# Attention of the second block's layers: heads in pairs, weights on the probabilities, outputs already turned

## The reference

```python
for l in range(2):
    h = rms_norm(x, norm_mix[l]) * (1 + sc_m) + sh_m
    (q_a, kc_a, vc_a, ks_a, vs_a, kw_a, vw_a, g_a, q_b, k_b, v_b, g_br) = split(h @ w_in[l])
    y_a = nsa_mixer(...)    # 8 query heads, 2 key/value groups, three branches:
    #   compressed: softmax(q @ k_c.T * 64**-0.5) @ v_c, 15 compressed keys (blocks of 32 tokens, stride 16)
    #   selected:   here all blocks are picked, so causal softmax(q @ k_slc.T * 64**-0.5) @ v_slc
    #   window:     window 512 > 256, so causal softmax(q @ k_win.T * 64**-0.5) @ v_win
    #   out = g[0] * o_c + g[1] * o_s + g[2] * o_w     (a sigmoid gate per token and head)
    y_b = moba_mixer(...)   # 8 heads with keys of their own, causal softmax over the 256 tokens
    merged = gate_a * (y_a @ w_up_nsa[l]) + gate_b * (y_b @ w_up_moba[l])
    x = x + g_m * (merged @ w_out[l])
    x = x + g_f * ffn(...)
```

## Time and profile before

| | us |
|---|---|
| median of 3 runs | 2434.91 (2433.66 to 2440.22) |
| the profiled execution | 2438.09 |
| its span | 2436.2 |
| TensorE busy | 2034.8 (84%) |
| VectorE busy | 411.6 (17%) |
| ScalarE busy | 325.4 (13%) |

### The profile page before, as it was taken

How to read it: one execution, slowest core, us unless ns; L and a number is a source line. 1 busy time by engine, 2 the same in 40 slices (tenths; PEclk the granted TensorE clock), 3 DMA queues, 4 the chain that set the end, 5 groups by cost and what they waited for, 6 DMA issues and landing times.

```text
span 2436.2 us, 28154 instructions
## 1 busy us (share of the span) xinstructions
PE 2034.8 (84%) x12190; PEld 1308.8 (54%) x12190; DVE 411.6 (17%) x1137; ACT 325.4 (13%) x737; POOL 0.2 (0%) x4
## 2 busy tenths in 40 slices
PE   6999997766656666666666699989999999899999
PEld 4468786421111111221111347878888658788887
DVE  4213343200000000000000114431000114411000
ACT  2232020200000000000000112431000122501000
POOL 0000000000000000000000000000000000000000
PEclk9999998888787788888788899899999999999999
DMA  9247577599999999999999954216334545045341
GB/s 327 77 165 271 197 267 285 210 422 427 430 428 429 428 428 429 428 429 427 430 428 429 411 195 157 86 70 242 138 127 168 192 138 208 1 173 207 136 175 35
DMA packets 147872, 648.48 MB, mean 266 GB/s; under 512 B 10645, under 2 KB 17410, under 8 KB 123016
## 3 DMA queue, kind: packets, MB, share of 16 engines
q1 hardware_dynamic: 140754, 643.00, 66.6%
q10 hardware_dynamic: 7030, 4.18, 0.7%
HBM read 646.10 MB, written 1.05 MB: 266 GB/s over the span
## 4 chain that ended last, share of the span: by engine, by line
PE 62%; DMA 31%; DVE 3%; ACT 2%; issue 1%; ACTq 1%; SPq 0%; DVEq 0%
DMA ring<-in_w_exp 31%; PE bank L806 27%; PE bank L820 6%; PE bank L2268 6%; PE bank L1601 4%; PE bank L1365 4%; PE bank L1616 2%; PE bank L577 1%; PE bank L839 1%; PE bank L684 1%; DMA ring<-in_w_branch_ml 1%; ACTq L346 1%; PE bank L1289 1%; PE bank L2074 1%; PE bank L2067 1%
## 5 line engine op out<-in xcount | busy, mean ns | idle before, releaser
L806 PE MATMUL bank<-hx,ring 128*128 128x256 f32 (+1 forms) x2944 | 655.1, 385 | 0.7 <-ACT hx L702 0.7
L806 PEld LDWEIGHTS bank<-hx,ring 128*128 128x128 f32 x2944 | 559.4, 190 | 93.3 <-issue 19.0
L1601 PE MATMUL bank<-ring,arena 128*32 128x512 f32 x1968 | 307.3, 759 | 201.8 <-DMA ring<-in_w_exp 191.4
L1601 PEld LDWEIGHTS bank<-ring,arena 128*32 128x32 f32 x1968 | 60.8, 124 | 430.9 <-DMA ring<-in_w_exp 310.0
L1616 PE MATMUL bank<-ring,arena 128*32 128x512 f32 x1008 | 159.9, 774 | 83.5 <-DMA ring<-in_w_exp 72.7
L820 PE MATMUL bank<-ring,hx 128*128 128x512 f32 (+1 forms) x384 | 152.9, 560 | 1.1 <-ACT hx L762 0.7
L2268 PE MATMUL bank<-arena,ring 128*128 128x256 f32 x704 | 152.4, 379 | 1.5 <-DVE arena L2301 1.5
L2268 PEld LDWEIGHTS bank<-arena,ring 128*128 128x128 f32 x704 | 133.6, 190 | 20.0 <-issue 1.9
L1616 PEld LDWEIGHTS bank<-ring,arena 128*32 128x32 f32 x1008 | 32.3, 130 | 193.6 <-DMA ring<-in_w_exp 114.5
L820 PEld LDWEIGHTS bank<-ring,hx 128*128 128x128 f32 x384 | 72.8, 190 | 80.1 <-issue 76.4
L1659 DVE COPY arena<-bank 128x256 f32<-128x256 f32 x16 | 6.8, 424 | 523.1 <-PE bank L1606 523.1
(11 more groups left out here) (370 smaller groups left out, 1542.3 us busy)
## 6 DMA issues: line engine op xcount, KB each, us to landing
ring<-in_w_exp SPq DMA_DIRECT2D x186, 2048.0 KB, 16.2
ring<-in_w_ada SPq DMA_DIRECT2D x36, 2048.0 KB, 12.4
ring<-in_w_in SPq DMA_DIRECT2D x29, 2048.0 KB, 9.1
ring<-in_w_ffn_in SPq DMA_DIRECT2D x20, 2048.0 KB, 7.9
ring<-in_w_ffn_out SPq DMA_DIRECT2D x10, 2048.0 KB, 7.8
ring<-in_w_out SPq DMA_DIRECT2D x6, 2048.0 KB, 12.0
arena<-in_w_exp SPq DMA_DIRECT2D x4, 2048.0 KB, 16.1
ring<-in_w_up_nsa SPq DMA_DIRECT2D x2, 2048.0 KB, 9.4
```

The source lines that it names most:

```text
L806: ins = pe.matmul(b[:, o:o + n], w[:, k, j * P:(j + 1) * P], h[:, k, :], start=k == 0, stop=k == KD - 1)
L1601: ins = pe.matmul(banks[s][32 * j:32 * j + 32, :], e_xe[:, 2 * t + kk, :], w[:, kk, 512 * j:512 * j + 512], start=t + kk == 0, stop=t + kk ...
```

## The change

- The unit is a pair of heads (`par` = 0, 1) of one branch: 12 units, the four pairs of the third branch first, then the other two branches of each pair.
- Keys are kept as pairs like the queries (`kT`). A head's scores are a matmul over its own 64 partitions; the two heads of a pair write to two banks.
- The scale 64**-0.5 is put into the query gains, so that `softmax_in` gives the exponential's bias directly (minimum of the negated scores); L2190 goes.
- New `normed(m)` on VectorE between `probs` and `turned`: reciprocal of the sums, times the gate, and four multiplies of the probabilities in place.
- `values` has the value columns as weights (64 columns) and the turned probabilities moving, so that the output is already turned. The two heads write the two halves of the partitions of one bank, and the three branches of a pair add up in that bank. `outputs` is a plain copy to `yT2`.
- One copy in six of the turned probabilities goes to VectorE (`on_dve`).
- The compressed scores are made turned (32 rows of keys a head, four pairs side by side), copied, turned back, softmaxed and weighted, turned again as one bank, and their values are added behind the window branch of each pair. The compressed values are made in four 32-partition copies.
- The opening's order is, on TensorE: scores(0), compressed scores, scores(1), their turn, turned(0), scores(2), turned(1), values(0), scores(3), turn of the compressed probabilities; on VectorE: softmax_in(0), softmax_in(1), compressed softmax, normed(0), softmax_in(2), compressed sums and weights, normed(1).
- `y2`, its turn and its copies go.

```diff
@@ heads
-                for par in range(2):
-                    lo, hi = 64 * par, 64 * par + 64
-                    s0 = par if q == 2 else 8 + par
-                    v.tensor_copy(kp[lo:hi, s0:s0 + 7:2, c * P:(c + 1) * P], bb[lo:hi]).then_inc(*DV.step("free " + key, f"kp{l}"))
+                s0 = 4 if q == 2 else 0
+                v.tensor_copy(kT[:, s0:s0 + 4, c * P:(c + 1) * P], b[:, :].rearrange("p (i t) -> p i t", i=4)).then_inc(
+                    *DV.step("free " + key, f"kT{l}"))
@@ TensorE
+    UNITS = [(2, p) for p in range(4, 8)] + [(b, p) for p in range(4) for b in range(2)]
+        def scores(m):
+            b = [bank(pe, f"s{l}_{m}{par}") for par in range(2)]
+            for c in range(NC):
+                for par in range(2):
+                    r = slice(64 * par, 64 * par + 64)
+                    o = slice(0, P) if c == 0 else slice(P, 3 * P)
+                    ins = pe.matmul(b[par][:, o], qT[r, pair, c * P:(c + 1) * P], kT[r, slot_, 0:(c + 1) * P],
+                                    start=True, stop=True)
+                    if c:
+                        ins.then_inc(*PE.step(f"full s{l}_{m}{par}"))
+        def turned(m):
+            for par in range(2):
+                b = bank(pe, f"pt{l}_{m}{par}")
+                pe.wait_ge(*at(f"N{l}_{m}{par}"))
+                for i in range(3):
+                    ins = pe.transpose(b[:, i * P:(i + 1) * P], sm[:, m % 3, par, i * P:(i + 1) * P], ident[:, :])
+                ins.then_inc(*PE.step(f"full pt{l}_{m}{par}"))
+        def values(m):
+            for par in range(2):
+                pe.wait_ge(*at(f"PT{l}_{m}{par}"))
+            for c in range(NC):
+                for par in range(2):
+                    o = b[64 * par:64 * par + 64, c * P:N]
+                    p_ = pt[:, m % 2, par, 0:N] if c == 0 else pt[:, m % 2, par, N:N + P]
+                    ins = pe.matmul(o, qkv[:, c, vcol[par]:vcol[par] + HD], p_, start=c == 0 and br != 1, stop=True,
+                                    skip_group_check=True)
+            ins.then_inc(*PE.step(f"V{l}_{m}"))
+            if br == 1:
+                for par in range(2):
+                    ins = pe.matmul(b[64 * par:64 * par + 64, 0:N], vc4[32 * pair:32 * pair + 16, pair // 2, :],
+                                    ptc[32 * pair:32 * pair + 16, par, :], start=False, stop=True, skip_group_check=True)
+                ins.then_inc(*PE.step("full " + key))
...
+        scores(0)
...
+        scores(1)
...
+        turned(0)
+        scores(2)
+        turned(1)
+        values(0)
+        scores(3)
...
+        for m in range(2, LAST):
+            turned(m)
+            values(m - 1)
+            if m == 4:
+                pe.wait_ge(*at(f"ptc{l}"))
+                pe.wait_ge(*at(f"cval ready{l}"))
+            if m + 2 <= LAST:
+                scores(m + 2)
+        turned(LAST)
+        values(LAST - 1)
+        values(LAST)
         pe_late(pe, 3 * l + 1)
-        pe.wait_ge(*at(f"attended{l}"))
...
@@ ScalarE
+        for m in range(2, LAST + 1):
+            copies(m - 2)
+            probs(m)
@@ VectorE
+        def normed(m):
+            v.wait_ge(*at(f"P{l}_{m}1"))
+            v.reciprocal(w, sums[:, m]).then_inc(*DV.step())
+            v.wait_ge(*DV.last())
+            if br < 2:
+                v.tensor_tensor(w, w, qkv[:, :, o:o + 4:3].rearrange("p c a -> p a c"), ALU.mult).then_inc(*DV.step())
+                v.wait_ge(*DV.last())
+            for par in range(2):
+                for c, (lo, hi) in enumerate(((0, P), (P, 3 * P))):
+                    x = sm[:, m % 3, par, lo:hi]
+                    v.tensor_scalar(x, x, w[:, par, c:c + 1], None, ALU.mult).then_inc(*DV.step(f"N{l}_{m}{par}"))
...
+        for m in range(2, LAST + 1):
+            if m + 1 <= LAST:
+                softmax_in(m + 1)
+            copies(m - 1)
+            normed(m)
+            outputs(m - 2)
```

More of the change, by code:

```diff
@@ L1893, in pe_compress @@
         b = bank(pe, f"cout{l}")
[L1894 to L1897, removed]
+        for g in range(2):
+            pe.matmul(b[0:15, g * HD:(g + 1) * HD], hidc[:, 0, 16 * g:16 * g + 15], cw2[:, l, 0, :], start=True, stop=True)
+        ins = pe_cvalues(pe, l, bank(pe, f"cval{l}"))
         ins.then_inc(*PE.step(f"full cout{l}"))
@@ L2062, in scores @@
[L2062 to L2103, removed]
-        turned(0)
[L2105 to L2118, removed]
-        pe_late(pe, 3 * l + 1)
-        pe.wait_ge(*at(f"attended{l}"))
[L2121 to L2124, removed]
-                for c in range(NC):
-                    j = 2 * kk + i
-                    ins = pe.transpose(b[:, (2 * i + c) * P:(2 * i + c + 1) * P], y2[:, c, j * P:(j + 1) * P], ident[:, :])
-            ins.then_inc(*PE.step("full " + key))
+        pe.wait_ge(*at(f"kT{l}"))
@@ new lines, in pe_attend @@
+        scores(0)
+        pe.wait_ge(*at(f"kct ready{l}"))
+        bc = [bank(pe, f"cs{l}{par}") for par in range(2)]
+        for p in range(4):
+            for par in range(2):
+                r = slice(64 * par, 64 * par + 64)
+                ins = pe.matmul(bc[par][32 * p:32 * p + 32, 0:N], kct[r, p // 2, :], qT[r, p, :], start=True, stop=True)
+        ins.then_inc(*PE.step(f"full cs{l}"))
+        scores(1)
+        pe.wait_ge(*at(f"scT{l}"))
+        b = bank(pe, f"ct{l}")
+        for par in range(2):
+            for c in range(NC):
+                o = (2 * par + c) * P
+                ins = pe.transpose(b[:, o:o + P], scT[:, par, c * P:(c + 1) * P], ident[:, :])
@@ new lines, in copies @@
+        def copies(m):
+            for par in range(2):
+                if on_dve(m, par):
+                    continue
+                key = f"pt{l}_{m}{par}"
+                act.wait_ge(*at("full " + key))
+                if m >= 2:
+                    act.wait_ge(*at(f"V{l}_{m - 2}"))
+                act.copy(pt[:, m % 2, par, :], bank_of(key)[:, 0:384]).then_inc(*AC.step("free " + key, f"PT{l}_{m}{par}"))
+        probs(0)
+        act.wait_ge(*at(f"full cs{l}"))
+        for par in range(2):
+            act.copy(scT[:, par, :], bank_of(f"cs{l}{par}")[:, 0:N]).then_inc(*AC.step(f"free cs{l}{par}", f"scT{l}"))
@@ new lines, in dve_attend @@
+        v.wait_ge(*DV.last())
+        v.tensor_reduce(m16, s16, AX, ALU.max).then_inc(*DV.step())
+        v.wait_ge(*DV.last())
+        v.tensor_tensor(s16, s16, spread(m16, 3, 16), ALU.subtract).then_inc(*DV.step(f"smC{l}"))
+        normed(0)
+        softmax_in(2)
+        v.wait_ge(*at(f"PC{l}"))
+        s4 = suC.rearrange("p a c h -> p (a c) h")
+        v.tensor_reduce(s4, s16, AX, ALU.add).then_inc(*DV.step())
+        v.wait_ge(*DV.last())
+        v.reciprocal(s4, s4).then_inc(*DV.step())
@@ L2238, in pe_gates2 @@
+        copies(LAST)
+        outputs(LAST - 1)
+        outputs(LAST)
     def pe_gates2(pe, l, t):
```

239 lines of the change are left out of this document (106 added, 133 removed).

## The result

The changed kernel takes 2458.35 us (median of five runs, 2455.21 to 2462.77) against 2436.06 (five runs, 2433.66 to 2440.22): a ratio of 1.0084, 95% interval 1.0067 to 1.0102. It is slower by 0.84%. The forecast was 2433 with a range of 2414 to 2456: it missed by 25 us and the median lies 2 us outside the range. The profiled execution of the changed kernel took 2455.21 (span 2453.4), 17.1 more than that of the kernel before (2438.09, span 2436.2).

The account below looks back on a forecast made before the run. TensorE, busy 84% of the span, was taken as the bound, so only its waits could give time. Layer 0 summed to 76.5 against 78.6, layer 1 to 76.5 against 76.5: 2436 profiled, 2433 median, range 2414 to 2456.

Parts of the forecast that it names:

- The place: Attention, from the compressed keys' turn to the mixer's first matmul: 78.6 us in layer 0, 76.5 in layer 1 before.
- The steady loop: Attention's head loop: TensorE and VectorE take turns, 4.98 us a pair at full clock; the loop gives nothing.
- What would show it: Signs in the profile after: alternating waits 5.0 to 5.3 us apart, values 0.7 us, mean clock 0.75 to 0.85.
- the forecast's caution: Loop's score matmuls: whether row groups overlap was unknown, so 0.87 us was taken, not 0.65, until the first head is full.
- The opening: Attention's start, up to normed(2): 17.1 us at full clock, plus 3 for slow matmuls, 20.1.
- The compressed values: Made in four quadrants, 20 instructions instead of 8: +0.9 us a layer.
- The clock: Attention loop: 38% of time at half clock, as in the expert stage, 0.6 us a pair more.
- the eight: Loop periods from pair 2 to pair 10: 41.1 us a layer, plus 4.7 for the clock.
- The end: Attention's close, from normed(10): 5.4 us a layer, plus 0.6 for the clock.
- Rival 2: Clock stays at half in the loop: 15.2 us a layer in place of 4.7, total 2457; chance 0.14.
- Rival 1: The clock holds in attention: 2423, or 2417 with a warm opening, 2414 with overlapping row groups too; chance 0.26.
- Rival 3: Loop's array halves don't run together (11 us), or each tiling switch drains, 0.16 us each (12 us, 2445); chance 0.16.

Follow-up runs that it names:

- run with six idle matmuls: The changed kernel with six unread 128-column matmuls put ahead of each pair's first transposes, where TensorE waits for VectorE: 2422.89 us, 0.9941 against the kernel before.
- run with scores first: The changed kernel with scores(m+2) put ahead of turned(m) and values(m-1) on TensorE in the loop, nothing else: 2386.25 us, 0.9788 against the kernel before.
- head-by-head run: The changed kernel with both score blocks of head 0 issued before those of head 1, instead of block by block: 2457.24 us, 1.0071 against the kernel before.
- Without the multiplies: The changed kernel with normed's four multiplies of the probabilities replaced by one small operation, so outputs are unscaled: 2443.76 us, 1.0021 against the kernel before.

## Why the prediction was wrong

*The place* was right: the change in time lies in the two stages in which it was looked for.

*The steady loop* came out to two hundredths: 4.98 forecast, 4.99 and 5.00 measured at full clock, with VectorE's wait ended by the scores and TensorE's by the multiply, in turn, as "What would show it" asked. The mechanism was right; that the sum came so near is partly luck. Errors cancel in it. In the period of layer 1 shown above: from the reciprocal to the end of the transposes 2.00 us (1.96 forecast), the values 0.80 (0.67), the scores and the hop behind them 0.99 (1.07), softmax_in 1.20 (1.28).

Two larger errors hide in these. The first is that the row halves run together, so that the forecast's caution (0.87 until the first head is ready, against 0.65 with overlap) was not needed: in both orders of issue the scores of the two heads start in pairs. The Trainium skill, "TensorE: Matmul & The Clock Gate", section "The mechanism" of Part 3, says that a weight load into another row group is pulled ahead of matmuls in flight, so that the tiles overlap; the trace agrees as to the overlap.

The second is that each change of tiling costs time, which the sum put at nothing. In the kernel before, at full clock, matmuls over the whole array (L2087, L2088) are followed by the late rows in column groups (L617):

```profile
1612.59 0.39 PE L2087 MATMUL bank<-arena,scr 128*128 128x64 f32 x2
1612.81 0.39 PE L2088 MATMUL bank<-arena,scr 128*128 128x64 f32 x2
1613.13 0.74 PE L617 MATMUL bank<-ring,small 128*32 128x128 f32 x18
```

From the first of two such matmuls to the next line's start are 0.22 us where the tiling stays, and 0.32 where it changes: 0.1 for the change. So the place in which the forecast saw no gap in the chain has one. In the loop, in the run with six idle matmuls:

```profile
1567.40 0.27 PE L2062 MATMUL bank<-ident,scr 128*128 128x128 f32 x1
1567.60 0.87 PE L2077 MATMUL bank<-scr,arena 128*64 128x256 f32 x8
1568.40 0.93 PE L2050 MATMUL bank<-arena 64*128 64x128 f32 x8
1569.26 0.60 PE L2059 MATMUL bank<-ones,ident 128*128 128x128 f32 x3
```

From the last transpose to the values are 0.20 us, where 0.11 is its own. From the values to the scores are 0.80 us, from the scores to the idle matmuls 0.86, where two halves side by side need 0.65 by the forecast's spacings. In the chain of a pair the first two changes and the slower start behind them cost 0.09, 0.15 and some 0.1: some 0.35 us. The third, back to the whole array, falls into the wait for VectorE. No run takes the tiling away by itself, so that the change of tiling is the cause is read from these places alone.

*The opening* was right: 20.1 forecast, 19.8 measured from the end of the keys' turn (1537.70) to pair 2's reciprocal (1557.50), at a clock of 0.66. *The compressed values* cost 0.15 and not 0.9: from line 1888's first matmul to the keys' turn 18.54 us before and 18.69 after.

*The clock* is the step that failed, in the size of its term: "The nearest row is the expert stage, busy for 552 of 860 us with regular waits: mean clock 0.81, so 38% of its time at half." From it came "0.6 a pair, 4.7 for the eight, 0.6 in the end". The price of a slow period was right: a pair at half clock was put at 7.0, and the eight periods from 1557.5 to 1614.1 take 56.6 us, 7.1 each. The share was wrong: with a mean clock of 0.58 nearly all of them were slow. So the eight take 56.6 where 45.8 was forecast (41.1 and 4.7), +10.8. The end takes 10.3 (to 1624.43) instead of 6.0, +4.3; its stretch from pair 10's transposes to the late rows is 9.3 us (1615.15 to 1624.43), and in the run with six idle matmuls, at full clock, 6.8 (1598.92 to 1605.74), of which 1.5 are idle matmuls: 5.3, so some 4 of the 4.3 are the clock too. 10.8 and 4.3, less 0.1 on the late rows and 0.3 on the opening, is within 0.1 the distance of 90.4 from the forecast's 75.6 without the compressed values. Layer 1 had a clock of 0.72 and is 4.5 us shorter.

The expert stage was near in its busy share (552 of 860 us, here 36.5 of 56.6) and its stops are of another kind: there TensorE waits for DMAs between runs of matmuls, here it stopped for 2.4 to 3.1 us in every pair of the loop but the first.

*The rivals.* Rival 2, the clock stays at half, held in layer 0 and for most of layer 1: 2457 by its own sum, 2458.35 measured; I gave it 0.14. Its term for the eight periods, 10.5 more than the forecast's, came out as 10.8 in layer 0 and less in layer 1, where two periods ran at full clock, so that the nearness of the total is partly luck. The row that spoke for it (a clock of 0.66 at the opening before) was in hand and was set below the expert stage's. Rival 1 is the run with six idle matmuls: 2422.89, its 2423. Rival 3 had two parts. Halves in series are refuted: the values take 0.80 us, not 1.30. A cost at each switch is there, near the price that it set (0.16 each): the lines above give some 0.35 us a pair for the two switches on the path. It did not make the kernel slower than forecast, since the rows' overlap, which the sum had left out, gave back a good part of it. The rule of the Trainium skill ("TensorEngine Tiling (Array Packing)", "Key Properties") is that changing the mode drains TensorE; the trace agrees, with 0.20 us instead of 0.11 between starts where the tiling changes.

*What the forecast left out.* It found that the order makes the engines take turns, priced it right, and concluded that the loop gives nothing. The run with scores first shows what the same parts can do: 2.8 to 3.3 us a pair instead of 5, at full clock. The forms that the change brings are sound; its order of issue is the loss.

*Open.* Why layer 1 had a clock of 0.72 against layer 0's 0.60, with the same instructions and the same stops, is not shown. It need not be a property of the layer: in the head-by-head run, with the same period, the stages took 88.1 and 89.7 us.

## What to carry to other kernels

When two engines feed each other, write down which instruction stands behind which wait on both queues before anything else: here matmuls that had all their inputs stood behind transposes that had not, and moving one call made the kernel nearly 3% faster than the change as it was made. Take the clock for a stage from stretches whose stops recur in the same way, not from those of the same busy share, and give the case in which it never recovers its own full sum. Filling TensorE's waits with idle matmuls shows within one run what the clock costs (36 us here), but the order of issue is the remedy: once it was right, the same fillers cost 5 us or brought nothing.

## What the runs showed of the hardware

The clock of this loop depended steeply on what filled its waits. With TensorE stopped for 2.4 to 3.1 us in each pair but the first the loop of layer 0 had 0.58; with two 128-column matmuls in the stop the stage had 0.72 (0.60 without them); with six the loop had 1.00, and TensorE's stop was down to 0.73 us, as the timeline of that run shows (idle time in brackets).

```profile
1566.60 1.07 PE L2062 MATMUL bank<-ident,scr 128*128 128x128 f32 x6 [0.73 <-DVE scr L2198]
```

Without the multiplies TensorE was busy for 30.1 of 46 us and the clock was 0.63, lower than the 0.82 of the expert stage with its 552 of 860.

At half clock TensorE looks busier for the same work (4.6 of 6.9 us in a pair), so a busy share read at half clock misleads about the stage:

```profile
1564.84:1571.78 6.94, 4.58 (x23) 2.85 (x23) 2.80 (x17) 2.56 (x10) 0.00 (x0) 0.65 0.00 0
```

```profile
1564.84 1.51 PE L2060 MATMUL bank<-ident,scr 128*128 128x128 f32 x6 [2.62 <-DVE scr L2196]
...
1569.55 0.29 DVE L2179 CUSTOM_DVE_ANT_0 scr<-bank,arena 128x128 f32<-128x128 f32 x1 [4.07 <-PE bank L2050]
```

Two views of one pair, the stretch and the timeline with the idle time in brackets: the transposes come after 2.62 us of idle TensorE, ended by the multiply, and softmax_in after 4.07 us of idle VectorE, ended by the scores. Each engine's stop is the other's work.

The mean clock of a stretch misleads too, since it counts the stops. The same pair in finer stretches, up to the values of the next:

```profile
1565.00:1569.00 4.00, 4.00 (x22) 2.65 (x21) 0.49 (x2) 0.96 (x2) 0.00 (x0) 0.50 0.00 0
1570.00:1571.00 1.00, 0.00 (x0) 0.00 (x0) 0.97 (x8) 0.77 (x3) 0.00 (x0) 1.00 0.00 0
1572.00:1573.00 1.00, 1.00 (x10) 0.61 (x10) 0.42 (x2) 0.77 (x4) 0.00 (x0) 1.00 0.00 0
1573.00:1576.00 3.00, 2.49 (x16) 1.27 (x12) 0.37 (x3) 0.27 (x1) 0.00 (x0) 0.51 0.00 0
```

TensorE was busy without a break and had half clock; then the clock was full while TensorE stood still; it was full for the next transposes, and at half again for the rest of that pair. So the pair has a mean clock of 0.65, and all its matmuls ran at half.
